# A two-block network on one core: both expert routings rewritten, and the recurrence's gate weights given two buffers

## What is computed

```python
def ec_moe(h, w_router, w_gate, w_up, w_down):            # first block, 16 experts
    cap = max(1, EC_CAPACITY * T // N_EXPERTS)            # 128
    affinity = jax.nn.softmax((h @ w_router), axis=-1)
    gate_vals, tok_idx = lax.top_k(jnp.swapaxes(affinity, 1, 2), cap)   # each expert takes its 128 best tokens
    ...
def hierarchical_moe(h, ...):                             # second block, 4 groups of 8 experts
    gp = jax.nn.softmax(hf @ w_group + b_group); gval, gidx = lax.top_k(gp, 1)
    el = hf @ w_router + b_router                         # of the chosen group
    ev, eidx = lax.top_k(el, 2)                           # two experts for each token
    dest = pstart[sorted_e] + arange(a_tot) - start[sorted_e]     # a slot for each of 2048 (token, expert)
    buf_tok = full(n).at[dest].set(token_id[order])       # slot -> token, the table that gathers read
    ...
def rg_lru(x, wa, ba, wx, bx, lam):                       # second block: 8 blocks of 128 channels
    r = sigmoid(block_diag_linear(x, wa, ba)); i = sigmoid(block_diag_linear(x, wx, bx))
    ...                                                   # then a linear recurrence over the tokens
```

## Time and profile before

| what | value |
|---|---|
| time, median of 3 runs | 4624.36 us (4620.41 to 4628.51) |
| time of the profiled execution | 4629.96 us |
| its span in the profile | 4628.0 us, 74180 instructions |
| busy share PE, DVE, ACT, POOL | 85%, 60%, 44%, 10% |
| mean granted TensorE clock | 0.913 |

### The profile page before, as it was taken

The page is one execution under the profiler, slowest core; times in us unless marked ns, Lnnn a source line. Parts: engine busy times, 40 slices in busy tenths (PEclk is TensorE's granted clock), DMA queues, the critical chain, the costliest instruction groups (busy, mean ns, idle before and its releaser), DMA issues. The chain is left out here.

```text
span 4628.0 us, 74180 instructions
## 1 busy us (share of the span) xinstructions
PE 3932.8 (85%) x30377; PEld 3129.9 (68%) x30377; DVE 2756.1 (60%) x4004; ACT 2041.1 (44%) x3434; POOL 468.4 (10%) x368
## 2 busy tenths in 40 slices
PE   6999877868897747999969889899899886599994
PEld 4888554458886526888758667677777654488883
DVE  4231254766665668999841577455443364599995
ACT  3111123645554316777731445455532232477772
POOL 0000012210002100111100243000000000111111
PEclk8999877989998878999979899899999998799997
DMA  5442212652223437999842233322143205799996
GB/s 205 140 157 81 107 51 71 200 148 78 73 81 125 150 146 295 389 397 395 336 168 91 99 108 108 106 73 67 44 133 122 87 14 206 287 414 409 412 410 248
DMA packets 376328, 836.79 MB, mean 181 GB/s; under 512 B 32639, under 2 KB 245151, under 8 KB 325558
## 3 DMA queue, kind: packets, MB, share of 16 engines
q1 hardware_dynamic: 357902, 782.00, 46.2%
q0 software_dynamic: 12032, 41.96, 2.9%
q10 hardware_dynamic: 6056, 8.08, 0.5%
HBM read 671.98 MB, written 159.96 MB: 180 GB/s over the span
## 5 line engine op out<-in xcount | busy, mean ns | idle before, releaser
L4636 DVE TENSOR_TENSOR moe_lo<-moe_raw,moe_hi 128x2048 fp32r<-128x2048 f32 x192 | 428.3, 2285 | 33.8 <-ACT moe_hi L4591 33.8
L515 PE MATMUL psum<-proj_hi,proj_w 128*128 128x512 f32 (+2 forms) x1440 | 409.9, 370 | 13.2 <-DVE proj_w L557 11.4
L4591 ACT ACTIVATE moe_hi<-moe_raw 128x2048 fp32r<-128x2048 f32 x192 | 356.8, 1910 | 41.1 <-PE psum L4552 41.1
L515 PEld LDWEIGHTS psum<-proj_hi,proj_w 128*128 128x128 f32 (+1 forms) x1440 | 259.2, 188 | 66.2 <-DVE proj_w L557 11.6
L515 PE MATMUL psum<-proj_lo,proj_w 128*128 128x512 f32 (+2 forms) x720 | 265.5, 369 | 0.0
L2893 DVE TENSOR_TENSOR moe_lo<-ahead_raw,moe_hi 128x2048 fp32r<-128x2048 f32 x96 | 218.9, 2288 | 22.6 <-ACT moe_hi L2841 22.5
L2893 DVE TENSOR_TENSOR moe_lo<-lT,moe_hi 128x2048 fp32r<-128x2048 f32 x96 | 218.8, 2288 | 21.7 <-ACT moe_hi L2841 21.7
L2841 ACT ACTIVATE moe_hi<-ahead_raw 128x2048 fp32r<-128x2048 f32 x96 | 184.1, 1919 | 70.0 <-PE psum L2794 70.0
L526 DVE COPY proj_out<-psum 128x512 f32<-128x512 f32 (+2 forms) x45 | 28.7, 638 | 310.0 <-PE psum L515 310.0
L2841 ACT ACTIVATE moe_hi<-lT 128x2048 fp32r<-128x2048 f32 x96 | 183.9, 1918 | 66.1 <-PE psum L2794 66.1
L1829 DVE COPY_PREDICATED chunks_X<-chunks_msk,psum 128x128 f32<-128x128 int32 x400 | 107.7, 302 | 143.1 <-PE psum L1579 128.2
(11 more groups left out here) (645 smaller groups left out, 9861.2 us busy)
## 6 DMA issues: line engine op xcount, KB each, us to landing
moe_raw<-in_w_gate_up SPq DMA_DIRECT2D x128, 1024.0 KB, 9.7
moe_raw<-in_w_down SPq DMA_DIRECT2D x64, 1024.0 KB, 7.7
lT<-in_w_gate SPq DMA_DIRECT2D x36, 1024.0 KB, 8.7
ahead_raw<-in_w_down SPq DMA_DIRECT2D x36, 1024.0 KB, 7.6
ahead_raw<-in_w_up SPq DMA_DIRECT2D x32, 1024.0 KB, 9.8
lT<-in_w_up SPq DMA_DIRECT2D x32, 1024.0 KB, 9.5
ahead_raw<-in_w_gate SPq DMA_DIRECT2D x28, 1024.0 KB, 9.1
lT<-in_w_down SPq DMA_DIRECT2D x28, 1024.0 KB, 7.7
```

The costliest lines, as they stand in the source:

```text
L515: ins = nc.tensor.matmul(bank[e * nch + c][0:width, 0:n], l, r, start=(k == 0 and i == 0), stop=(k == KD - 1 and i == 2))
L4591: nc.scalar.activation(hi[:, n % R], raw[:, n % RAW], ACT.Copy).then_inc(s["hi_ready"], 1)
L4636: nc.vector.tensor_tensor(lo[:, n % R], raw[:, n % RAW], hi[:, n % R], ALU.subtract).then_inc(s["lo_ready"], 1)
```

## The change

**`route1`.** `wr` is padded to 32 columns and zeroed by POOL first; SP's load waits for that. Contraction piece k goes to the column tile k % 4 (32 columns of the array, 32 partitions of the bank), so four partial sums stand side by side in `lT` (128 partitions); they are turned whole, and DVE adds the four parts with two reductions. The second half is evicted by DVE. The affinities are laid out as two halves of 512 tokens on 64 partitions (16 experts and 16 rows of padding for each half), and the 16 rounds take the best 128 of each half. The two sorted lists are then merged: PE multiplies the second by a reversed identity (`rev`), and DVE takes the larger of value i of the first and value 127-i of the second, with its index. Five semaphores are new.

**`route2`.** `wr` is padded to 64 columns and zeroed by POOL, as is `br`, ahead of SP's loads; the pieces go to two column tiles of 64; two DVE reductions add the parts. The table of slots no longer goes through HBM: DVE splits a slot into block and row, makes `at_block` (128x768: equals block, times the token's number) and `at_row` (128x2048: equals row), and PE sums the products of the 16 pairs in 16 matmuls (128x128 by 128x48). The scatters, the clearing of `slot_tok` and the stage `slot_tokens` are gone.

**`qkv_and_lru`.** `lw` has two buffers, with a semaphore each; block b+1 is loaded at step R_AT[b], once block b-1's second product is done.

The constant table `cst` is 224 columns wider.

```diff
-                sp.dma_start(wr[:, :, :], w_router.rearrange("(k p) e -> p k e", p=P)).then_inc(w_in, 16)
+                sp.wait_ge(blank, 1)
+                with nc.allow_non_contiguous_dma("narrow matrix"):
+                    sp.dma_start(wr[:, :, 0:E1], w_router.rearrange("(k p) e -> p k e", p=P)).then_inc(w_in, 16)
...
             @block.gpsimd
             def _(pool):
+                nc.gpsimd.memset(wr[:, :, :], 0.0).then_inc(blank, 1)
                 nc.gpsimd.memset(zero[:, :], 0.0).then_inc(zeroed, 1)
+                nc.gpsimd.memset(ex[:, :, E1:S], 0.0).then_inc(padded, 1)
...
                 for c in range(2):
                     for k in range(KD):
-                        last = nc.tensor.matmul(bank[c][0:E1, :], wr[:, k, :], hT[:, k, c * BANK:(c + 1) * BANK],
-                                                start=(k == 0), stop=(k == KD - 1))
+                        g = k % 4 * S
+                        last = nc.tensor.matmul(bank[c][g:g + S, :], wr[:, k, :], hT[:, k, c * BANK:(c + 1) * BANK],
+                                                start=(k < 4), stop=(k >= 4), skip_group_check=True)
                     last.then_inc(l_mm, 1)
-                pe.wait_ge(l_ev, 2)
                 for i in range(NT):
-                    last = nc.tensor.transpose(bank[2][:, i * E1:(i + 1) * E1], lT[:, i * P:(i + 1) * P], ident[0:E1, 0:E1])
+                    if i == 0:
+                        pe.wait_ge(l_ev, 1)
+                    elif i == 4:
+                        pe.wait_ge(l_ev2, 1)
+                    last = nc.tensor.transpose(bank[2 + i // 4][:, i % 4 * P:(i % 4 + 1) * P], lT[:, i * P:(i + 1) * P], ident)
                 last.then_inc(tr, 1)
                 pe.wait_ge(p_ready, 1)
+                pe.wait_ge(padded, 1)
                 for i in range(NT):
...
                 pe.wait_ge(ixf_ready, 1)
-                nc.tensor.transpose(bank[5][:, 0:E1], va[:, :], ident[0:E1, 0:E1])
-                nc.tensor.transpose(bank[5][:, E1:2 * E1], ixf[:, :], ident[0:E1, 0:E1]).then_inc(fin_mm, 1)
+                for n in range(2):
+                    last = nc.tensor.transpose(bank[6][:, n * 2 * S:(n + 1) * 2 * S], vi[:, n, :], ident[0:2 * S, 0:2 * S])
+                last.then_inc(fin_mm, 1)
+                pe.wait_ge(listed, 1)
+                for h, order in enumerate((ident, reverse)):
+                    last = nc.tensor.matmul(bank[7][:, h * 2 * E1:(h + 1) * 2 * E1], order, lists[:, :, h * S:h * S + E1],
+                                            start=True, stop=True)
+                last.then_inc(pair_mm, 1)
 
             @block.scalar
             def _(act):
...
+                dve.wait_ge(l_mm, 2)
+                nc.vector.tensor_copy(lT[:, BANK:], bank[1][:, :]).then_inc(l_ev2, 1)
                 dve.wait_ge(tr, 1)
-                lp = bank[2][:, 0:NT * E1].rearrange("p (n e) -> p n e", e=E1)
-                dve.wait_ge(chain, link(nc.vector.tensor_reduce(mx[:, :], lp, AX_X, ALU.max)))
-                nc.vector.tensor_tensor(lg[:, :, :], lp, mx[:, :].unsqueeze(2).to_broadcast([P, NT, E1]), ALU.subtract)\
+                for h in range(2):
+                    parts = bank[2 + h][:, :].rearrange("p (n g e) -> p n e g", n=4, g=4)[:, :, 0:E1, :]
+                    last = link(nc.vector.tensor_reduce(lg[:, 4 * h:4 * h + 4, :], parts, AX_X, ALU.add))
+                dve.wait_ge(chain, last)
...
-                for r in range(CAP // 8):
-                    v8, i8, a, b = va[:, 8 * r:8 * r + 8], ix[:, 8 * r:8 * r + 8], af[r % 2], af[(r + 1) % 2]
+                for h in range(2):
+                    dve.wait_ge(chain, link(nc.vector.tensor_copy(af[0][h * S:(h + 1) * S, :], bank[4 + h][0:S, :])))
+
+                for n in range(CAP // 8):
+                    v8, i8, a, b = vi[:, 0, 8 * n:8 * n + 8], ix[:, 8 * n:8 * n + 8], af[n % 2], af[(n + 1) % 2]
                     dve.wait_ge(chain, link(nc.vector.max(v8, a[:, :])))
                     link(nc.vector.max_index(i8, v8, a[:, :]))
                     dve.wait_ge(chain, link(nc.vector.match_replace(b[:, :], v8, a[:, :], -1.0)))
-                nc.vector.tensor_copy(ixf[:, :], ix[:, :]).then_inc(ixf_ready, 1)
+                nc.vector.tensor_copy(vi[:, 1, :], ix[:, :]).then_inc(ixf_ready, 1)
                 dve.wait_ge(fin_mm, 1)
-                nc.vector.tensor_copy(gates[:, :], bank[5][:, 0:E1]).then_inc(fin, 1)
-                nc.vector.tensor_copy(idx[:, 0:E1], bank[5][:, E1:2 * E1]).then_inc(fin, 1)
...
-                nc.vector.tensor_copy(idx[:, E1:E1 + 1], bank[5][:, E1:E1 + 1]).then_inc(fin, 1)
+                nc.vector.tensor_copy(lists[:, :, :].rearrange("p n e -> p (n e)"), bank[6][:, 0:4 * S]).then_inc(listed, 1)
+                dve.wait_ge(pair_mm, 1)
...
+                                                                       ALU.add, ALU.add)))
+                nc.vector.tensor_copy(idx[:, 0:E1], best[:, :]).then_inc(fin, 1)
+                nc.vector.tensor_copy(idx[:, E1:E1 + 1], best[:, 0:1]).then_inc(fin, 1)
 
...
                         for n, src in enumerate((wa, wx)):
-                            sp.dma_start(lw[:, n, :], src[b]).then_inc(l["w_in"], 16)
+                            sp.dma_start(lw[:, b % 2, n, :], src[b]).then_inc(l[f"w_in{b % 2}"], 16)
...
                             load_block(b + 1, "x")
-                        if n == I_AT[b] + 1:
-                            sp.wait_ge(l["i_mm"], b + 1)
+                        if n == R_AT[b]:
+                            if b:
...
                     for c_ in range(2):
-                        ins = nc.tensor.matmul(bank[4 + c_][:, :], lw[:, m, :], xc(b)[:, c_ * BANK:(c_ + 1) * BANK], start=True, stop=True)
+                        ins = nc.tensor.matmul(bank[4 + c_][:, :], lw[:, b % 2, m, :], xc(b)[:, c_ * BANK:(c_ + 1) * BANK], start=True, stop=True)
...
             @block.gpsimd
             def _(pool):
+                nc.gpsimd.memset(wr[:, :, :], 0.0).then_inc(s["blank"], 1)
+                nc.gpsimd.memset(br[:, :], 0.0).then_inc(s["blank"], 1)
                 nc.gpsimd.memset(zero[:, :], 0.0).then_inc(s["zeroed"], 1)
-                pool.wait_ge(s["cleared"], 16)
-                pool.wait_ge(s["dest_ready"], 1)
-                for k in range(2):
-                    for i in range(NT):
-                        pool.indirect_dma_start(out=slot_tok[:, :],
-                                                out_offset=bass.IndirectOffsetOnAxis(ap=dest[:, k * NT + i:k * NT + i + 1], axis=0),
-                                                in_=tok[:, i:i + 1], in_offset=None).then_inc(placed, 16)
-                pool.wait_ge(placed, 16 * 2 * NT)
 
             @block.tensor
...
+                        g = k % 2 * C
+                        last = nc.tensor.matmul(bank[c][g:g + C, :], wr[:, k, :], hT[:, k, c * BANK:(c + 1) * BANK],
+                                                start=(k < 2), stop=(k >= KD - 2), skip_group_check=True)
                     last.then_inc(s["l_mm"], 1)
-                pe.wait_ge(s["l_ev"], 2)
                 for i in range(NT):
-                    last = nc.tensor.transpose(bank[2][:, i * W:(i + 1) * W], lT[:, i * P:(i + 1) * P], ident[0:W, 0:W])
+                    if i % 4 == 0:
+                        pe.wait_ge(s["l_ev"], i // 4 + 1)
+                    last = nc.tensor.transpose(bank[5 + i // 4][:, i % 4 * P:(i % 4 + 1) * P], lT[:, i * P:(i + 1) * P], ident)
...
+                pe.wait_ge(s["placed"], 1)
+                for j in range(2 * NT):
+                    last = nc.tensor.matmul(bank[7][:, 0:NB], at_row[:, j, :], at_block[:, j, :], start=(j == 0), stop=(j == 2 * NT - 1))
+                last.then_inc(s["slots_mm"], 1)
...
                 dve.wait_ge(s["tr"], 1)
-                step(V.tensor_copy(lg[:, :, :].rearrange("p n w -> p (n w)"), bank[2][:, 0:NT * W]))
+                for h in range(2):
+                    parts = bank[5 + h][:, :].rearrange("p (n g w) -> p n w g", n=4, g=2)[:, :, 0:W, :]
+                    step(V.tensor_reduce(lg[:, 4 * h:4 * h + 4, :], parts, AX_X, ALU.add))
...
                     step(V.tensor_reduce(df[:, k, :], G_[:, :, :], AX_X, ALU.add))
-                V.tensor_copy(dest[:, :], df[:, :, :].rearrange("p k n -> p (k n)")).then_inc(s["dest_ready"], 1)
+                places = df[:, :, :].rearrange("p k n -> p (k n)")
+
+
+                step(V.tensor_scalar(bl[:, 0, :], places, 1.0 / P, -(P - 1) / (2.0 * P), ALU.mult, ALU.add))
+                step(V.tensor_scalar(bl[:, 1, :], bl[:, 0, :], ROUND, None, ALU.add))
+                step(V.tensor_scalar(bl[:, 1, :], bl[:, 1, :], -ROUND, None, ALU.add))
+                step(V.scalar_tensor_tensor(bl[:, 2, :], bl[:, 1, :], -float(P), places, ALU.mult, ALU.add))
+                step(V.tensor_tensor(at_block[:, :, :], iota128[:, 0:NB].unsqueeze(1).to_broadcast([P, 2 * NT, NB]),
```

(12 more changed lines are left out.)

112 lines of the change are left out of this document (57 added, 55 removed).

## The result

The changed kernel takes 4575.65 us (median of 4 runs, 4569.52 to 4587.66); the kernel before, with its runs beside them, 4625.94. The ratio is 0.9885, with a 95% interval of 0.9872 to 0.9898: 50.3 us less. Forecast were 4571.0 us in a range of 4559 to 4587, that is 53.4 less. A second set of five runs gave 4576.28 against 4626.46, ratio 0.9892 (0.9871 to 0.9913).

What follows compares the result with a forecast made beforehand. No single engine was taken as the bound (PE 85% of the span); the change touches stretches where PE stands still. Terms -29.8-18.3-5.6+0.3 = -53.4 from the median 4624.36 gave 4571.0 us, range 4559 to 4587.

Steps and rivals of the forecast that it cites:

- selection and merge: First routing: 48 DVE passes over 512 tokens instead of 1024, 0.53 us less each, -25.6; merging the two lists +2.4.
- logits, first: First routing: 16 products on four column tiles run as 4 rounds, 6.2 us instead of 16.78, -10.6.
- first logits' start, behind SP's load: First routing: SP's weight load waits for POOL's fill of `wr`, which comes late after semaphore clears, +2.6 us.
- turning back: First routing, between logits and softmax: eviction, four turns and two reductions, 2.4 us with gaps, +1.1.
- slot table: Second routing: table built by DVE and 32 PE passes (5.9 us, mostly low clock), 11.7 us instead of 26.7, -15.0.
- gather behind SP: After second routing: POOL clears 17 semaphores instead of 3, gather 0.9 us later; costs 0.9 or nothing, put at +0.4.
- gate weights: Recurrence's stage: of PE's 17.6 us wait in two places, only DVE's own waits come back, 2.5 and 3.1, -5.6 us.
- Rival A: Logits in both routings: column tiles don't run side by side, their 17.7 us gain is lost, 4588.7 us; chance 0.08.
- D: Logits: alternating column groups empties the array, kernel slower than before, 4644 us at 1.3 us a pass; chance 0.01.
- B: Recurrence's stage: the gate stall moves entirely to the next waits on ACT, 4576.6 us; chance 0.09.
- C: Recurrence's stage: the whole gate stall comes back, with the clock, 4555.2 us; chance 0.07.
- the 0.3 for the wider constants: Kernel's first loads: the wider constants are 115 KB at 427 GB/s while the loads saturate the queues, +0.3 us.

Runs made afterwards that it cites:

- tile order: Changed kernel with the first routing's contraction pieces in the order 0,4,1,5,2,6,3,7; one profile, the group of 32 logit passes 1.4 us shorter than 6.37.
- clears-later run: Changed kernel with POOL's clearing of each routing's semaphores moved behind the next stage's first gather; one profile, first expert product 1.2 us sooner, second routing 1.1 to 1.2.

## Why the prediction was right

By its own steps, from the two profiled executions:

| step | forecast | measured |
|---|---|---|
| selection and merge | -25.6 + 2.4 | -23.0 |
| logits, first | -10.6 | -10.4 |
| first logits' start, behind SP's load | +2.6 | +2.8 |
| turning back | +1.1 | +0.9 |
| softmax's reduction to the first pass | 0 | -0.8 |
| clears ahead of the gather | +0.3 | +0.6 |
| gather's landing | 0 | -0.4 |
| first routing (D1) | -29.8 | -30.3 |
| logits, second, with their start and the reductions | -7.1+2.9+0.5 | -6.7+2.7+0.5 |
| slot table | -15.0 | -13.7 |
| gather behind SP | +0.4 | +1.2 |
| second routing (D3) | -18.3 | -16.0 |
| gate weights (D2) | -5.6 | -4.0 |

**The selection** came out by the slope from plain DVE instructions: the three kinds of pass have the same price an element. **The softmax** was put at nothing and gave 0.8: PE's eight turns behind it took 1.05 us at a granted clock of 1.00 and not 1.88 at 0.50. That is no scatter: the four kernels with the old routings have 1.88, nine of the ten with the new ones 1.05, and the one whose clock rose soonest in the logits (tile order) 1.63 at 0.59. I had not followed the clock past the logits.

**The column tiles** gave all they could. At 1.2 GHz a step of four passes takes 0.85 us, as a single pass did (7 of them started in 5.2 us). Rival A is out, and so is D. The Trainium skill's measured 2.38 times for three column tiles (TensorE: Matmul & The Clock Gate, Part 3) was not the figure here: four tiles ran four passes in the time of one, and the forecast that kept to the rows was 0.2 us off.

**The slot table** was mis-sized by 1.3 us: PE's 32 passes were put at 5.9 between bounds of 3.5 and 7.1, and took 7.06. The clock was 0.50 all along. I had left room for it to rise, against the row that priced the low clock; that row decided rightly, 0.22 each. The Trainium skill (TensorE: Matmul & The Clock Gate, LDWEIGHTS (loading the stationary operand)) gives a load P / 1.2 ns for P columns, with no term for the clock; an estimate from that formula is 107 ns for 128 columns and 3.4 us for the 32 passes. The trace at the low clock has twice that.

**The gather** was the other miss, 1.2 us and not 0.4. 0.9 of it is the later issue (1.81 us behind SP's first load, not 0.89), 0.3 a slower landing. I split the 0.9 us between two cases, as the profile did not seem to say whether it or the weights set the first product. The clears-later run shows that the gather does: the first product moves with it. The row of PE's turn, with the gather named as what ended its wait in both kernels, could have been read for that.

**The gate weights** gave 4.0 of the 5.6 forecast, and the reason is the one forecast: DVE's chain bounds what comes back. I had counted each of DVE's waits in the stretch as a gain (2.5 and 3.1). In the first place 1.2 was kept, since DVE's chain started only 0.24 us sooner at the step after the stall and PE's lead, 8.3 us at the next gate product, was down to 4.0 at the fourth turn behind the stall and to 1.2 at the fifth. In the second place the lead at ACT's roots grew from 1.5 to 3.1, that is by 1.6 and not 3.1, and stayed there to the last gate; 0.9 more came up behind it, which I can't place. So the mechanism was right and the gain of each place mis-sized by a factor of about two. B (nothing) was nearer in single runs (0.7 in one) than C, which the trace of no run bears out.

Between the 53.4 us forecast and the 50.3 of the medians stand the table, the gather and the gates with 3.7, and D1 gave 0.5 back; the 0.3 for the wider constants shows in none of the three distances. D1's agreement is partly luck: the softmax and the gather's landing, both put at nothing, made up for what the starts and clears cost.

## What to carry to other kernels

When a long stall is removed, ask which engine's chain the waiting engine would meet next, and size the gain by that chain's own waits, not by the stall; then look at the chain, for that is where the next 15 us lay (a reciprocal of 1024 columns that an identity replaces). Price halved work by the slope of plain instructions of the same engine, and put passes behind a long pause of PE (11.3 us here) at the low clock without a discount. Compare stages between the same instructions and not whole executions: here stages that no edit touched moved by 17 us between runs.

## What the runs showed of the hardware

- Column tiles don't need neighbours on different tiles. With both pieces of a tile next to each other in the list, the 32 passes still ran four at a time, in steps of 0.85 us at 1.2 GHz and 0.43 at 2.4.
- POOL takes 0.065 to 0.08 us to clear a semaphore (1.10 us for 17, 1.58 for 20), and 20 of them stood between an index and its gather. Moving them paid 1.2 us.
- PE's clock rose 2.7 us after the logits' start in one run and 5.5 in another, with the same eight steps. The length of a pause alone did not tell whether it fell: after idle products that ended 3.38 us ahead of the next work it was back at 1.2 GHz, and with a pause of 1.53 us it was not; but in the first routing it was low after a pause of 1.94 us in the kernel before and high after one of 2.72 us in the changed one.
- Products of 48 columns in fp32r cost the same per pass as in float32 (0.226 and 0.221 us, both at 1.2 GHz): the load of 128 columns is nearly the whole price (3.49 of 3.61 and 6.90 of 7.06 us), and one pass in place of two is half the time.
